# Second branch of a two-layer hybrid block: head scores over 128 zero-padded rows instead of 32, stabiliser product over 128 rows instead of 64

## The reference, cut to what matters

```python
def mlstm_chunkwise(q, k, v, i_pre, f_pre, state):
    ...
        b = jnp.cumsum(jax.nn.log_sigmoid(fc), axis=-1)
        dlog = jnp.where(tril, b[..., :, None] - b[..., None, :] + ic[..., None, :], -jnp.inf)
        g = b + m[..., None]
        mj = jnp.maximum(g, dlog.max(-1))
        s = jnp.exp(dlog - mj[..., None]) * jnp.einsum('bhjd,bhsd->bhjs', qc, kc)
        inter = jnp.exp(g - mj)
        num = jnp.einsum('bhjs,bhsv->bhjv', s, vc) + inter[..., None] * jnp.einsum('bhvd,bhjd->bhjv', C, qc)
        den = s.sum(-1) + inter * jnp.einsum('bhd,bhjd->bhj', n, qc)
        h = num / jnp.maximum(jnp.abs(den), jnp.exp(-mj))[..., None]
```

## Time and profile before

| | us |
|---|---|
| median of 3 runs (3119.08 to 3123.03) | 3120.57 |
| the profiled execution, device time | 3124.59 |
| its span, first to last instruction | 3120.9 |
| PE busy in the span | 2719.1 (87%) |
| DVE, ACT, POOL busy | 849.4, 600.2, 170.2 |
| second branch's loop, layer 0 (315.40 to 410.57) | 95.17 |
| second branch's loop, layer 1 (1990.14 to 2058.21) | 68.07 |

### The profile page before, as it was taken

How to read it: one execution, slowest core, us unless ns; L and a number is a source line. 1 busy time by engine, 2 the same in 40 slices (tenths; PEclk the granted TensorE clock), 3 DMA queues, 4 the chain that set the end, 5 groups by cost and what they waited for, 6 DMA issues and landing times.

```text
span 3120.9 us, 38826 instructions
## 1 busy us (share of the span) xinstructions
PE 2719.1 (87%) x15968; PEld 1465.1 (47%) x15968; DVE 849.4 (27%) x1967; ACT 600.2 (19%) x1170; POOL 170.2 (5%) x178
## 2 busy tenths in 40 slices
PE   6868997899998899899898587997899889888884
PEld 3335555674445544344343333555778753332233
DVE  1132235431112521111112513234531242111114
ACT  3232213221002011111111223223221201111111
POOL 0000000000000011111110000000000011111100
PEclk8999588899998799999999799778999989999897
DMA  6010002241200569999996501001233189999993
GB/s 271 20 54 7 27 27 103 93 187 54 81 27 21 217 263 420 419 395 404 376 409 246 240 21 54 34 28 60 79 137 135 47 341 388 425 422 413 415 401 150
DMA packets 74559, 617.38 MB, mean 198 GB/s; under 512 B 17678, under 2 KB 17678, under 8 KB 32016
## 3 DMA queue, kind: packets, MB, share of 16 engines
q1 hardware_dynamic: 50192, 564.52, 44.5%
q0 software_dynamic: 24192, 50.39, 4.3%
HBM read 604.87 MB, written 47.71 MB: 209 GB/s over the span
## 4 chain that ended last, share of the span: by engine, by line
PE 82%; DVE 7%; issue 4%; DMA 4%; ACT 3%; SPq 0%; POOLq 0%; ACTq 0%; DVEq 0%; POOL 0%
PE bank L1701 19%; PE bank L1716 9%; PE bank L1187 8%; PE bank L286 6%; PE bank L356 3%; PE bank L1202 3%; PE bank L1192 3%; PE bank L1691 2%; PE bank L601 2%; PE bank L587 2%; DMA arena<-expert_rows 2%; PE bank L377 1%; PE bank L397 1%; PE bank L905 1%; PE bank L920 1%
## 5 line engine op out<-in xcount | busy, mean ns | idle before, releaser
L1701 PE MATMUL bank<-ring,arena 128*64 128x512 f32 (+1 forms) x1648 | 587.4, 631 | 102.5 <-issue 97.7
L1701 PEld LDWEIGHTS bank<-ring,arena 128*64 128x64 f32 (+1 forms) x1648 | 203.4, 159 | 425.2 <-issue 424.2
L1187 PE MATMUL bank<-normed,ring 128*128 128x512 f32 (+1 forms) x768 | 255.5, 486 | 0.0
L1701 PE MATMUL bank<-branches,arena 128*64 128x512 f32 (+1 forms) x528 | 249.3, 628 | 0.0
L1879 DVE TENSOR_TENSOR arena<-bank,arena 128x256 f32<-128x256 f32 x83 | 35.2, 424 | 706.3 <-ACT arena L1803 706.3
L1625 POOL DMA_INDIRECT arena<-hidden_rows,block_slots x81 | 82.2, 1015 | 2502.7 <-DVE block_slots L1454 1895.0
L286 PE MATMUL bank<-normed,ring 128*128 128x512 f32 x448 | 197.3, 600 | 0.0
L1187 PEld LDWEIGHTS bank<-normed,ring 128*128 128x128 f32 x768 | 145.9, 190 | 102.2 <-issue 92.3
L1716 PE MATMUL bank<-ring,arena 128*64 128x512 f32 (+1 forms) x560 | 163.4, 597 | 1.3 <-DVE arena L1885 1.3
L1803 ACT ACTIVATE arena<-bank 128x256 f32<-128x256 f32 x83 | 31.9, 384 | 688.9 <-PE bank L1701 688.9
L1716 PE MATMUL bank<-arena 128*64 128x512 f32 (+1 forms) x528 | 139.9, 604 | 1.1 <-ACT arena L1806 1.1
(11 more groups left out here) (427 smaller groups left out, 3707.2 us busy)
## 6 DMA issues: line engine op xcount, KB each, us to landing
ring<-in_wexp SPq DMA_DIRECT2D x96, 2048.0 KB, 19.6
ring<-in_wst SPq DMA_DIRECT2D x54, 2048.0 KB, 8.4
branches<-in_wexp SPq DMA_DIRECT2D x34, 2048.0 KB, 22.0
ring<-in_wexp SPq DMA_DIRECT2D x66, 1024.0 KB, 21.7
arena<-in_wexp SPq DMA_DIRECT2D x64, 1024.0 KB, 21.6
arena<-expert_rows SPq DMA_DIRECT2D x12, 2048.0 KB, 7.5
ring<-in_wst SPq DMA_DIRECT2D x4, 1536.0 KB, 11.3
hidden_rows<-arena SPq DMA_DIRECT2D x6, 512.0 KB, 2.9
```

Of the source, the lines that this page charges most:

```text
L1187: last = nc.tensor.matmul(ps[2 * (n % 4)][:, c0:], wg[:, k, i * P:(i + 1) * P], H[:, k, c0:], start=(k == 0), stop=(k == KD - 1))
L1701: last = nc.tensor.matmul(ps[2 + s][r0:r1, :], XT_[:, s, k * P + r0:k * P + r1], wt[:, k, :], start=(k == 0), stop=(k == KD - 1))
```

## The change

The change gives each head a query array of its own, 128 partitions high, in which only the head's 32 partitions hold its queries and the other 96 are zero. The score product then contracts all 128 partitions of zk with that array, without a tile position. The stabiliser product contracts 128 partitions, of which the upper 64 of RT's plane are set to zero (the constant "sel" has zeros there too). The result of every product is the same. The number and the order of PE's products don't change, nor do their columns.

```diff
-        zq, zk, so = arena(0, T), arena(512, T), arena(2048, 2, T)
+        zk, so = arena(512, T), arena(2048, 2, T)
+        zq = [arena(at, T) for at in (0, 1024, 1536, 16448)]
...
-            pe.wait_ge(ml["zev"], l * ML["zev"] + 2)
+            pe.wait_ge(ml["zev"], l * ML["zev"] + 5)
...
-                nc.tensor.matmul(ps[MB_BANK[u % 2]][:, :], cn("sel", P, u * P)[0:64, :], RT[0:64, 1, :], start=True, stop=True).then_inc(ml["mb"], 1)
+                nc.tensor.matmul(ps[MB_BANK[u % 2]][:, :], cn("sel", P, u * P), RT[:, 1, :], start=True, stop=True).then_inc(ml["mb"], 1)
...
-                q = slice(32 * h, 32 * h + 32)
-                nc.tensor.matmul(ps[QK_BANK[p % 3]][:, j0:j1], zk[q, s * P:(s + 1) * P], zq[q, j0:j1],
-                                 start=True, stop=True, tile_position=(32 * h, 0)).then_inc(ml["qk"], 1)
+                nc.tensor.matmul(ps[QK_BANK[p % 3]][:, j0:j1], zk[:, s * P:(s + 1) * P], zq[h][:, j0:j1],
+                                 start=True, stop=True).then_inc(ml["qk"], 1)
...
-            for j, dst in enumerate((zq, zk)):
-                act.wait_ge(ml["z"], l * ML["z"] + j + 2)
-                nc.scalar.activation(dst, ps[j][:, :], ACT.Copy, scale=float(MLQK) ** -0.5 if j == 0 else 1.0).then_inc(ml["zev"], 1)
+            act.wait_ge(ml["z"], l * ML["z"] + 2)
+            act.wait_ge(ml["zm"], l * ML["zm"] + 1)
+            for h in range(MLH):
+                q = slice(32 * h, 32 * h + 32)
+                nc.scalar.activation(zq[h][q, :], ps[0][q, :], ACT.Copy, scale=float(MLQK) ** -0.5).then_inc(ml["zev"], 1)
+            act.wait_ge(ml["z"], l * ML["z"] + 3)
+            nc.scalar.activation(zk, ps[1][:, :], ACT.Copy).then_inc(ml["zev"], 1)
...
             ch.add(nc.vector.memset(VA[:, :, :, ML_V:V_W], 1.0))
+            ch.add(nc.vector.memset(RT[64:128, 1, :], 0.0))
+            for h in range(MLH):
+                last = nc.vector.memset(zq[h], 0.0)
+                if h < MLH - 1:
+                    ch.add(last)
+            last.then_inc(ml["zm"], 1)
```

More of the change, by code:

```diff
@@ L517, in build @@
         dns, h_ms, h_rs = arena(16384, 2, TT), arena(16400, TT, MLH), arena(16416, TT, MLH)
-        ml, ML = signals("ml", z=7, zev=2, oev=2, vev=2, ab=1, ln=1, mb_in=1, e=2, ra=3, mb=8, mbs=8, dg=8,
+        ml, ML = signals("ml", z=7, zm=1, zev=5, oev=2, vev=2, ab=1, ln=1, mb_in=1, e=2, ra=3, mb=8, mbs=8, dg=8,
                                                     qk=36, d=36, s=36, pv=8, h=8, hs=2, sq=2, rd=2, so=2, rs=1, hn=2, ht=2, out=2)
```

## The result

The changed kernel takes 3030.46 us (median of 3 runs, 3029.15 to 3031.60) against 3120.57 us. The ratio is 0.9711, 95% interval 0.9697 to 0.9725: 90 us or 2.9% faster. The forecast was 3034.

What follows compares the result with a forecast made beforehand. TensorE bounds the kernel, its clock halved in the second branch's loops by low products. Loops of 73.0 + 2.5 + 4 = 79.5 us save 83.7, projections behind 3.0: 86.7 off 3120.57, forecast 3034, range 3024 to 3072.

Steps and rivals of the forecast that it cites:

- What keeps the clock: Second branch's loops: TensorE, though busy, runs at 1.2 GHz because of 64- and 32-row products; streamed full rows hold full clock.
- Columns and weight loads at full clock: Both loops: scores, stabiliser and value products take 41.7 us in layer 0 and 31.3 in layer 1, 73.0 together.
- Steps between heights, waits at the start, hand-offs: Both loops: 2.5 us of waits for DVE at the starts, 4 us for hand-offs and group steps (0.25 a unit).
- Behind the loops: The first 32 projection instructions after each loop fall from 15.16 and 15.66 us to 13.9, giving 3.0 us.
- Added work at nothing: Ahead of the loops: five MEMSETs and the extra query copies are hidden, cost 0; uncovered, 4.3 us a layer.
- Rival B: In the loops the clock comes and goes around the value products: 3070 us, range 3050 to 3090; chance 0.11.
- Rival C: Rows don't set the loops' clock; only steps between groups go, 10 to 20 us: 3101 to 3110; chance 0.05.
- Rival D: Rival C holds and uncovered added work delays the loops, 8.6 us: 3129; chance 0.03, its half-covered case 0.03.
- the 64-row group at 588.14 us: Eight end-to-end products of 64 rows and 512 columns, said to take the clock from 1.00 down to 0.50.

Runs made afterwards that it cites:

- The probe: 32 products a layer ahead of each loop: 32-row on four row groups in the kernel before, 3136.8 us; 128-row in the changed kernel, 3082.3 us.

## Why the prediction was right

The mechanism of the prediction held; the term that was sized wrong is small.

- *What keeps the clock.* Read from the attention, which is 65% busy at 1.00, and the loops, which are 99% busy at 0.53. The clock is 1.00 after. That it is the height and not something else in the edit is shown from both sides: without it in the scores the gain is gone (3115.1 us), and with full-height fillers beside untouched 32-row scores the clock holds. That it is not the steps between heights is shown by the scores of 64 and of 32 rows, 1.00 and 0.55 in the loop of layer 1 with the same steps.
- *Columns and weight loads at full clock.* 73.0 us were counted, and the two loops take 76.5.
- *Steps between heights, waits at the start, hand-offs.* 6.5 us were taken on top of the columns and weight loads, 3.5 are there. The first value product starts 7.76 us into the loop of layer 0 (321.75 - 313.99), forecast 7.8, so the start was sized right. The mis-sized term is the 0.25 us a unit for hand-offs: a unit takes 5.25 us for 5.2 of work. The loops gave 86.8 us where 83.7 were forecast; these 3.1 us are about what lies between 3034 and 3030.5.
- *Behind the loops.* 3.0 us forecast, 2.9 measured.
- *Added work at nothing.* Five MEMSETs and three copies in each layer are hidden. DVE waits 0.30 us for ACT ahead of the gate sums where it had waited 3.22, and three times as many zeros more did not move the loops' starts.
- *Rival B*, a clock that comes and goes, did not show at 128 rows: it is 1.00 in both loops. With 64-row scores the clock did fall in one of them.
- *Rival C* fell. The Trainium skill, TensorE: Matmul & The Clock Gate, section The HAM clock gate, says that the clock follows how busy TensorE is; the traces of these loops do not agree. TensorE was busy for 94.62 of 95.17 us at 0.53, and is for 42.57 of 43.56 at 1.00. The fillers could hardly raise a busy time that was full (87.03 of 87.03 us), and the clock went to 1.00. *Rival D* fell with it: there is far more cover than the added work needs.
- Two arguments of the prediction were too weak. It weighed the Trainium skill's advice to put small products side by side against the padding by what the trace of before showed, and in the loops of that trace no such products stand side by side. The probe shows that they do run so. And it took the 64-row group at 588.14 us as a second place where height brings the clock down, but passed over the same group in the other direction, at 484.66 us, which ran at 1.00 from end to end:

```profile
484.66 3.70 PE L866 MATMUL bank<-arena,small_weights 64*128 64x512 f32 x8
```

  A group that short proves little either way; the third branch with 128 rows, and the experiments on the scores, carry the argument.

What stays open is a loop that takes four heads at once on four row groups. The scores would take 29.6 / 4 = 7.4 us instead of 29.6 in the two loops, an estimate from the probe and from the columns counted; against that stand the steps to and from the value products, 0.2 to 0.33 us for each product of another height, four score banks at a time where there are three, and the open question whether such a loop holds the clock. It was not tried. Open too is what settles whether the clock falls at 64 rows.

## What to carry to other kernels

Where TensorE is busy all the time and its granted clock is still 0.5, look at the height of its products. With contractions of 32 or 64 rows that run one at a time, padding to 128 with zeros adds no columns, and here it nearly doubled the speed of everything in the stretch, the untouched products included. Height is not the only cause: the 128-row products of 64 columns in the earlier trace rows stayed at 0.50. Pad first the products that make up most of the streaming, as the scores did here; half height held the clock in one loop and lost it in the other. Once the clock holds and TensorE is still the bound, each column spared counts in full, unless another engine is waited for right behind, as in the third branch.

## What the runs showed of the hardware that I had not expected

- Four 32-row products on separate row groups and banks ran at 3.9 times the rate of 128-row products one after another (64 instructions in 7.15 us, against 27.63), at a granted clock of 1.00.
- With 64-row scores the same program held 1.00 in one loop (39.70 us) and fell to 0.50 after 33 us in the other (71.96 us), and its executions spread over 18 us.
- The third branch's 64-row group in its first direction can run at either level, and it starts behind the same wait of 6.27 us and the same four 128-row instructions in both kernels. In the changed kernel it takes 7.19 us, with a granted clock of 0.50 over all of it, though TensorE is busy throughout:

```profile
430.42 7.19 PE L876 MATMUL bank<-arena,small_weights 64*128 64x512 f32 x8
```

  In the kernel before the same eight instructions took 3.70 us, at a clock of 1.00. With 128 rows (the run on the third branch) the group started at 0.50 as well, but the clock rose within it, and it took 4.47 us. Why the two kernels differ here stays open. Of the 5.7 us that this group and the two behind it lose, 4.2 come back in a shorter wait for DVE (3.89 us instead of 8.07), which leaves the 1.5 us of the section on the result.
- At full clock a product of another height than its neighbours costs 0.21 us (64-row scores) to 0.33 us (64-row stabiliser) more, the steps ahead of it and behind it together; groups of equal height but different width follow each other without a step.
- A weight load whose 128 columns are one column read with a step of zero gives the right result (the stabiliser product of the run on the third branch).
